# Gate units of a PEER layer: a scaled one-hot made by one engine instead of two

## The reference, cut to what matters

```python
idx = e1 * PEER_NKEYS + e2                 # 128 expert numbers per token, e1 and e2 below 128
g = jax.nn.softmax(top, axis=-1)           # their gates
hid = jax.nn.gelu(jnp.einsum('td,thkd->thk', xb, expert_down[idx]))
y = jnp.einsum('thk,thkd->td', g * hid, expert_up[idx])
```

## Time and profile before

| | us |
|---|---|
| median of 3 runs | 3475.59 |
| lowest and highest | 3459.72 to 3480.33 |
| the profiled execution | 3480.13 |
| its span on the core | 3478.0 |

### The profile page before, as it was taken

How to read it: one execution, slowest core, us unless ns; L and a number is a source line. 1 busy time by engine, 2 the same in 40 slices (tenths; PEclk the granted TensorE clock), 3 DMA queues, 4 the chain that set the end, 5 groups by cost and what they waited for, 6 DMA issues and landing times.

```text
span 3478.0 us, 47895 instructions
## 1 busy us (share of the span) xinstructions
PE 3361.5 (97%) x18808; PEld 3050.2 (88%) x18808; DVE 1818.9 (52%) x3788; ACT 1391.9 (40%) x2516; POOL 1853.0 (53%) x1071
## 2 busy tenths in 40 slices
PE   7998899999999899999999998999999999999999
PEld 6755789999999898899988887999999999889998
DVE  4525218995886444444422311699587744444443
ACT  3334223336786333333333322333477733333332
POOL 3400436776677545555544553477767773555553
PEclk9956899999999999999989998999999999999999
DMA  2200124667999888888732222366699998888884
GB/s 106 97 13 1 67 85 163 223 201 269 385 383 394 318 296 320 309 325 318 282 109 97 85 83 81 121 209 199 217 359 383 387 359 304 319 309 318 324 309 165
DMA packets 234302, 808.21 MB, mean 232 GB/s; under 512 B 21088, under 2 KB 70240, under 8 KB 225376
## 3 DMA queue, kind: packets, MB, share of 16 engines
q1 hardware_dynamic: 160352, 536.69, 43.4%
q0 software_dynamic: 73728, 268.47, 20.0%
HBM read 702.32 MB, written 102.76 MB: 231 GB/s over the span
## 4 chain that ended last, share of the span: by engine, by line
PE 84%; DMA 6%; ACT 4%; POOL 3%; DVE 2%; issue 2%; SPq 0%; DVEq 0%; ACTq 0%
PE banks L233 23%; PE banks L234 22%; PE banks L235 22%; PE banks L956 3%; PE banks L920 2%; DMA arena<-down,side 2%; ACT arena L783 2%; POOL weights_lo L213 2%; PE banks L491 2%; PE banks L480 1%; PE banks L248 1%; PE banks L249 1%; PE banks L250 1%; PE banks L280 1%; ACT weights_hi L207 1%
## 5 line engine op out<-in xcount | busy, mean ns | idle before, releaser
L213 POOL TENSOR_TENSOR weights_lo<-raw_ring,weights_hi 128x1024 fp32r<-128x1024 f32 x498 | 1273.0, 2558 | 1121.8 <-ACT weights_hi L207 1120.3
L233 PE MATMUL banks<-operand_hi,weights_hi 128*128 128x384 f32 (+1 forms) x4800 | 1676.5, 349 | 29.0 <-POOL weights_lo L213 14.7
L234 PE MATMUL banks<-operand_lo,weights_hi 128*128 128x384 f32 (+1 forms) x4800 | 1650.1, 344 | 0.0
L235 PE MATMUL banks<-operand_hi,weights_lo 128*128 128x384 f32 (+1 forms) x4800 | 1649.7, 344 | 0.0
L233 PEld LDWEIGHTS banks<-operand_hi,weights_hi 128*128 128x128 f32 x4800 | 906.9, 189 | 118.9 <-issue 73.3
L234 PEld LDWEIGHTS banks<-operand_lo,weights_hi 128*128 128x128 f32 x4800 | 906.9, 189 | 29.3 <-issue 3.6
L235 PEld LDWEIGHTS banks<-operand_hi,weights_lo 128*128 128x128 f32 x4800 | 906.0, 189 | 28.3
L207 ACT CAST weights_hi<-raw_ring 128x1024 fp32r<-128x1024 f32 x624 | 652.9, 1047 | 676.9 <-PE banks L235 580.0
L1121 DVE TENSOR_TENSOR residual<-residual,banks 128x384 f32<-128x384 f32 x256 | 141.9, 554 | 654.8 <-PE banks L235 645.3
L812 ACT ACTIVATE arena<-banks 128x384 f32<-128x384 f32 x256 | 126.0, 492 | 523.3 <-PE banks L235 472.4
L783 ACT ACTIVATE arena<-operand_hi,side 128x128 f32<-128x128 f32 x768 | 235.4, 393 | 51.3 <-DVE operand_hi L1085 46.6
(11 more groups left out here) (175 smaller groups left out, 2798.0 us busy)
## 6 DMA issues: line engine op xcount, KB each, us to landing
raw_ring<-weight_tiles SPq DMA_DIRECT2D x624, 512.0 KB
hid_scratch<-arena SPq DMA_DIRECT2D x64, 768.0 KB
gate_scratch<-arena SPq DMA_DIRECT2D x24, 2048.0 KB
arena<-hid_scratch SPq DMA_DIRECT2D x32, 1536.0 KB
arena<-gate_scratch SPq DMA_DIRECT2D x32, 1536.0 KB
arena<-up,side POOLq DMA_INDIRECT x146
residual<-x_t SPq DMA_DIRECT2D x2, 1024.0 KB, 6.7
arena<-key_t SPq DMA_DIRECT2D x2, 1024.0 KB, 5.1
```

The source lines that it names most:

```text
L213: eng.tensor_tensor(wl[:, b, :], raw[:, n % RING, :], wh[:, b, :].bitcast(F32), ALU.subtract).then_inc(done, 1)
L233: pe.matmul(out, w_hi, x_hi[:, c, :], start=start and c == 0, stop=False)
L234: pe.matmul(out, w_hi, x_lo[:, c, :], start=False, stop=False)
L235: last = pe.matmul(out, w_lo, x_hi[:, c, :], start=False, stop=stop and c == DC - 1)
```

## The change

DVE writes `oh2` itself. For each of a unit's 8 tokens one `tensor_scalar` operation compares the iota row in PSUM (128 columns) with the token's e2 column and multiplies by its g column, both read as per-partition scalars. The comparison of 1024 elements into `eq2`, ACT's `scale` with its eight multiplications, and the semaphores `equals` and `g_scaled` are gone. PE waits on `onehots` alone, which `oh1`'s comparison raises after the eight new operations.

```diff
@@ peer_act @@
-            def scale(u):
-
-                act.wait_ge(s.equals, was["equals"] + u + 1)
-                for t in range(8):
-                    last = act.mul(oh2[:, u % 2, t, :], eq2[:, u % 2, t, :].bitcast(F32), columns_t[:, 2, 8 * u + t:8 * u + t + 1])
-                last.then_inc(s.g_scaled, 1)
@@
                 for u in units_at(h):
-                    scale(u)
                     if u:
                         evacuate(u - 1)
@@ peer_pe, gates_of @@
                 pe.wait_ge(s.onehots, was["onehots"] + u + 1)
-                pe.wait_ge(s.g_scaled, was["g_scaled"] + u + 1)
@@ peer_dve @@
                 if u >= 2:
                     dve.wait_ge(s.gate_made, was["gate_made"] + 2 * u - 2)
-                dve.tensor_tensor(eq2[:, u % 2], iota8, of_tokens(1, 8 * u), ALU.is_equal).then_inc(s.equals, 1)
+                for t in range(8):
+                    tk = 8 * u + t
+                    dve.tensor_scalar(oh2[:, u % 2, t, :], ps[:, 4, 0:KEYS], columns_t[:, 1, tk:tk + 1], columns_t[:, 2, tk:tk + 1],
+                                      ALU.is_equal, ALU.mult)
                 dve.tensor_tensor(oh1[:, u % 2], iota8, of_tokens(0, 8 * u), ALU.is_equal).then_inc(s.onehots, 1)
                 dot()
                 dot()
             while dots[0] < P:
                 dot()
-            dve.wait_ge(s.g_scaled, was["g_scaled"] + UNITS)
             dve.memset(side[:, 0:1088], 0.0).then_inc(s.z_cleared, 1)
```

More of the change, by code:

```diff
@@ L152, in build @@
         PEER = {"keys_loaded": 16, "q_copied": PQ, "scored": PQ, "score_copied": PQ, "top_shifted": 1, "top_exp": 1, "routed": 2,
-                "turned": 1, "turn_copied": 1, "equals": UNITS, "g_scaled": UNITS, "experts": 1, "gelu_done": PDOWN, "onehots": UNITS,
+                "turned": 1, "turn_copied": 1, "experts": 1, "gelu_done": PDOWN, "onehots": UNITS,
                 "gate_made": 2 * UNITS, "gate_copied": 2 * UNITS, "dotted": P, "hid_g": 1, "w_made": 1, "w_turned": 1, "w_copied": 1,
@@ L163, in peer_sems @@
             s.dve, s.top_shifted, s.top_exp, s.routed = (sem(tag + k) for k in ("_dve", "_top_shifted", "_top_exp", "_routed"))
-            s.turned, s.turn_copied, s.equals, s.g_scaled, s.experts = (
-                sem(tag + k) for k in ("_turned", "_turn_copied", "_equals", "_g_scaled", "_experts"))
+            s.turned, s.turn_copied, s.experts = (sem(tag + k) for k in ("_turned", "_turn_copied", "_experts"))
             s.gelu_done, s.onehots, s.gate_made, s.gate_copied = (sem(tag + k) for k in ("_gelu_done", "_onehots", "_gate_made", "_gate_copied"))
@@ L650, in build @@
         oh1 = oph_flat[:, 4096:6144].rearrange("p (b t i) -> p b t i", b=2, i=KEYS)
-        eq2 = oph_flat[:, 6144:8192].rearrange("p (b t i) -> p b t i", b=2, i=KEYS)
         picked = opl_flat[:, 4096:6144].rearrange("p (h k a) -> p h k a", h=PH, k=TOPK)
```

## The result

| | before | after |
|---|---|---|
| median of 12 runs, us | 3468.42 | 3488.41 |
| lowest to highest | 3435.84 to 3480.33 | 3482.61 to 3499.05 |
| the profiled execution | 3480.13 | 3485.79 |

The ratio is 1.0059, with a 95% interval of 1.0038 to 1.0080: 0.6% slower, 20 us in the medians. In a later series of rounds the changed kernel had 1.0041 (1.0027 to 1.0054) against the kernel before. The forecast was 3470 us, a little faster; the measured time lies in its range, on the other side of the kernel before.

What follows compares the result with a forecast made beforehand. PE bounds the unit stretches, with 23.6 us of gaps from ACT. Half kept, 10 us, less 1 us a layer for DMA: 8 us less, 3472 or 3468 us by base, called 3470; range 3453 to 3503 us.

Steps and rivals of the forecast that it cites:

- The bound before: Two stretches of PEER units: PE first, DVE, ACT and DMA close; ACT ends PE's gaps, at most 23.6 us to win.
- Removed from ACT: Eight multiplications a unit, 2.46 us, 236 us over 96 units; counts only where PE waited for ACT, nearly all gaps gone.
- Added to DVE: Eight 128-column operations replace one comparison in each unit: DVE's unit goes from 4.54 to 5.48 us, hardly keeping up with PE.
- p: Pitch, start to start, of DVE's eight new small operations: taken as 0.26 us, bounds 0.20 and 0.35 us.
- the rival: DVE becomes the bound from the fourth unit on: p = 0.32 us, unit 5.96 us, about 3495 us; chance 0.35.
- The break-even: Last unit's start in a layer stays at 1093.2 us if p = 0.296 us; each 0.01 us more costs 3.6 us a layer.
- The prediction's own sign for DVE as the bound: In the unit stretches, PE's waits put down to DVE's one-hot line or its successor sum to over 24 us.
- I keep half of the gaps: With DVE at 99% of PE's pace, late gathers keep part of PE's gaps: 5 us a layer won, 10 in all.
- The DMA rival: DMA engines, 0.98 busy in the units, give nothing back; gaps return as gather waits or later: 3476 us, chance 0.15.
- The rule on small tiles: Fixed part of an instruction is paid by each small tile, 512 elements or more advised: 1 us a unit lost on DVE.

Runs made afterwards that it cites:

- e3: The kernel before with ACT scaling one token of a unit instead of eight from a layer's third unit on, DVE unchanged: 3445.0 us, ratio 0.9918.
- e1: The changed kernel with the multiplication by g left out of the eight operations, so each reads one per-partition scalar: 3458.9 us, ratio 0.9966 against the kernel before.
- e8: The changed kernel with the eight small operations replaced by two of 1024 elements, a comparison and a multiplication from SBUF: 3496.4 us, ratio 1.0063 against the kernel before.

## Why the prediction was wrong

**The bound before: right.** PE was first, its gaps came from ACT, and their removal is worth 28 us (e3). That the change can win no more than the 23.6 us that the waits summed to was too low a bound: it left out that PE works at a higher granted clock without the gaps (8.9 us less busy in e3).

**Removed from ACT: right.** PE's waits for ACT vanish in the changed kernel.

**Added to DVE: the step that failed.** "I take p = 0.26 us, by the row it is nearest to" mis-sized the one term that decides. The one-scalar price was exact (e1: 0.26 us, unit 5.48 us forecast and 5.48 measured). The eight operations have two, and p is 0.32 us. The text had the right value beside it, from what the first scalar adds in the rows, and put it in the rival. The trace of the kernel before had the price at 128 columns as well (352 against 292 ns, under e1). For an operand that the nearest rows lack, the price of the operand they have should have been added to the term and not kept for the range.

**The break-even: right in kind.** p = 0.296 us was to be the point; 0.26 gave -12 us (e1) and 0.32 gave +20. The rival's sum was 3495 us, from 8.2 us a layer and some gather waits; measured were 3488 and 8.3 us in the first stretch, 4.3 in the second. The prediction's own sign for DVE as the bound, waits of PE over 24 us, came true with 30.4.

**"I keep half of the gaps": right in the time, partly by luck.** With p = 0.26 the forecast was 8 us less, and e1 gave 12 less. But of the 23.6 us of waits 17.0 were left there (9.1 and 7.9), not half, and 2.7 us of the stretches' gain lie in the first layer and 8.0 in the second.

**The DMA rival: wrong.** With PE's gaps gone the engines moved 398 GB/s in the stretch (e3). The 28.2 us won in the stretches are all of the 28 us in the time.

**The rule on small tiles: right in size, but not what turned the sign.** The Trainium skill (VectorE: DVE Perf Modes, "The TRN2 errata") speaks of a fixed part paid by each small tile. The prediction counted by it a loss of 1 us a unit on DVE. e1 pays 0.94 us (5.48 - 4.54) and is 12 us under the kernel before, yet 14 us over e3, which doesn't pay it. With the second scalar the loss is 1.43 us (5.97 - 4.54), and DVE had room for about 1 us under PE's 5.5 (259.7 us / 47 units in e3).

## What to carry to other kernels

Work can be moved to an idle engine up to the pace of the stage and no further: reckon its whole turn per step (here 4.54 us, then 5.97) against the bound's (5.5), and near the crossing half a microsecond per step turned 12 us of gain into 20 us of loss (e1 and the changed kernel). Leave some reserve: with DVE at 5.48 us against 5.5 half of the 28 us was gone already. Where one engine's relief is worth something and the other has some room, move a part: 3 of 8 tokens gave 17 us, all 8 cost 20. Price an instruction by its own operands; a row that lacks one of them is a lower bound. And count a gap of PE with the slower work behind it.

## What the runs showed of the hardware

- A second per-partition scalar costs DVE 0.06 us at 128 columns from PSUM (339 ns with one, 399 with two, e1), and a first one as much at 128 columns from SBUF (352 ns against 292 with a number in the program). A second arithmetic step cost nothing (692 ns against a copy's 693, 512 columns from PSUM).
- After a gap of 3.92 us PE's granted clock was 0.50 and 16 gates took 3.78 us instead of 1.95. Over the two stretches of the changed kernel the same instructions kept PE busy 531.7 us, of the kernel before 525.5, of e3 516.6.
- The faster SBUF form was the slower choice: 336 ns in the median against 399, yet the kernel is 1.2% slower, since single operations took up to 2.7 us beside POOL's subtraction. Beside its gather issues alone a unit's eight kept their 2.13 us. A multiplication with both inputs in SBUF took up to 3.6 us against 1.22 (e8).
- With more asked of them the DMA engines gave more: a busy share of 0.98 at 370 GB/s before was no limit, 1.03 came with 398 GB/s (e3).
